# A hybrid attention block on one Trainium2 core: the first block re-ordered from its projections to its masks

## The reference

```python
proj = rms_norm(h, norm_mix) @ w_in          # q, k, v of attention, rw (15 tiles), two gates
y_sb = stick_breaking_attention(q, k, v)     # 8 heads of 64
rw   = token_shift(rw, mu)                   # p + (previous row - p) * mu
r, kr, vr, w_lo, a_lo, g_lo = split(rw)
decay = exp(-exp(-softplus(-(w0 + tanh(w_lo) @ w_up)) - 0.5))
a = sigmoid(a0 + a_lo @ a_up);  g = sigmoid(g_lo) @ g_up
kk = kr * k_k;  kk = kk / max(norm(kk per head), 1e-12)
kr = kr * (1 + (a - 1) * k_a)
y_rw = rwkv7_recurrence(r, decay, kr, vr, kk, a)   # here: blocks of 16, 128, 128 rows
y_rw = (group_norm(y_rw) + sum(r * kr * r_k) * vr) * g
merged = sigmoid(gate_sb) * (y_sb @ w_sb_out) + sigmoid(gate_rw) * (y_rw @ w_rw_out)
h = h + merged @ w_out                        # then the feed-forward part, then block two
```

## Time and profile before

| | us |
|---|---|
| median of 3 runs (2523.31 to 2527.19) | 2525.39 |
| the profiled execution's own time | 2529.52 |
| its span in the profile | 2527.6 |
| PE busy | 2458.6 (97%) |
| DVE busy | 1724.1 (68%) |
| ACT busy | 1252.1 (50%) |
| POOL busy | 537.2 (21%) |

### The profile page before, as it was taken

The page is one execution under the profiler, slowest core; times in us unless marked ns, Lnnn a source line. Parts: engine busy times, 40 slices in busy tenths (PEclk is TensorE's granted clock), DMA queues, the critical chain, the costliest instruction groups (busy, mean ns, idle before and its releaser), DMA issues.

```text
span 2527.6 us, 43738 instructions
## 1 busy us (share of the span) xinstructions
PE 2458.6 (97%) x17339; PEld 2225.9 (88%) x17339; DVE 1724.1 (68%) x3045; ACT 1252.1 (50%) x2676; POOL 537.2 (21%) x423
## 2 busy tenths in 40 slices
PE   7899999999999999999999999999999999999997
PEld 6868998998789999999788878779999999888886
DVE  4647454446669777888777555759876888777556
ACT  5442235445555544444555555555454444555553
POOL 3601134555268300000000001448500000000000
PEclk9989999999999999999999999999999999999999
DMA  5400045565245655555787664335666565787664
GB/s 175 140 12 26 26 145 181 183 186 156 68 134 168 183 184 183 186 180 184 225 246 231 193 206 151 108 102 166 184 184 183 181 185 180 221 245 233 198 196 146
DMA packets 148073, 421.06 MB, mean 167 GB/s; under 512 B 15904, under 2 KB 49056, under 8 KB 147488
## 3 DMA queue, kind: packets, MB, share of 16 engines
q1 hardware_dynamic: 144080, 405.34, 52.2%
q0 software_dynamic: 2192, 8.99, 1.0%
q10 hardware_dynamic: 1600, 3.96, 0.5%
HBM read 400.40 MB, written 17.83 MB: 165 GB/s over the span
## 4 chain that ended last, share of the span: by engine, by line
PE 87%; DVE 6%; DMA 3%; ACT 3%; issue 1%; POOL 0%; ACTq 0%; DVEq 0%; SPq 0%
PE pb L430 86%; DMA raw<-in_vT 3%; PE pb L439 1%; ACT arena L1122 1%; DVE arena L1575 1%; ACT hi L1110 1%; DVE arena L1578 1%; DVE lo L1585 1%; ACT L1122 0%; DVE WL L2270 0%; DMA H<-in_x 0%; DVE arena L2243 0%; DVE arena L1657 0%; DVE arena L1634 0%; DVE H L1575 0%
## 5 line engine op out<-in xcount | busy, mean ns | idle before, releaser
L1110 ACT CAST hi<-raw 128x512 fp32r<-128x512 f32 x1402 | 814.7, 620 | 387.7 <-DMA raw<-in_vT 193.2
L430 PE MATMUL pb<-HTh,hi 128*128 128x256 f32 (+1 forms) x2968 | 857.8, 289 | 0.1
L430 PE MATMUL pb<-HTl,hi 128*128 128x256 f32 (+1 forms) x2968 | 842.3, 284 | 0.0
L430 PE MATMUL pb<-HTh,lo 128*128 128x256 f32 (+1 forms) x2968 | 842.0, 284 | 0.0
L2306 POOL TENSOR_TENSOR lo<-raw,hi 128x512 fp32r<-128x512 f32 x383 | 516.5, 1372 | 595.8 <-ACT hi L1110 595.2
L1585 DVE TENSOR_TENSOR lo<-raw,hi 128x1024 fp32r<-128x1024 f32 x464 | 565.4, 1219 | 83.8 <-ACT hi L1110 83.8
L430 PEld LDWEIGHTS pb<-HTh,hi 128*128 128x128 f32 x2968 | 570.2, 192 | 2.7 <-DVE arena L1575 0.6
L430 PEld LDWEIGHTS pb<-HTl,hi 128*128 128x128 f32 x2968 | 570.6, 192 | 1.0
L430 PEld LDWEIGHTS pb<-HTh,lo 128*128 128x128 f32 x2968 | 569.8, 192 | 0.0
L430 PE MATMUL pb<-hi,WH 128*128 128x512 f32 x1112 | 434.7, 391 | 6.6 <-DVE WL L2270 6.5
L430 PE MATMUL pb<-lo,WH 128*128 128x512 f32 x1112 | 433.5, 390 | 0.0
(11 more groups left out here) (194 smaller groups left out, 2272.0 us busy)
## 6 DMA issues: line engine op xcount, KB each, us to landing
raw<-in_uT SPq DMA_DIRECT2D x256, 512.0 KB, 3.7
raw<-in_vT SPq DMA_DIRECT2D x256, 512.0 KB, 4.3
raw<-in_w_ffn_in SPq DMA_DIRECT2D x44, 512.0 KB, 4.0
raw<-in_wq SPq DMA_DIRECT2D x32, 512.0 KB, 3.6
wk<-kept SPq DMA_DIRECT2D x128, 128.0 KB, 4.3
raw<-in_w_in SPq DMA_DIRECT2D x24, 512.0 KB, 3.7
raw<-in_w_ffn_out SPq DMA_DIRECT2D x22, 512.0 KB, 4.4
raw<-in_w_gate SPq DMA_DIRECT2D x16, 512.0 KB, 3.5
```

Of the source, the lines that this page charges most:

```text
L430: return e.matmul(o, l, r, start=start, stop=stop)
L1110: e.copy(u.hi[k], u.half[k]).then_inc(*s.up("hi", ("hi", g)))
```

## The change

Nothing is computed by another method except two roots and two scalings: the square root and reciprocal of the key norm and of group norm become exp(-0.5 ln(x)) on ACT, and the decays' factor -exp(-0.5) moves from a DVE instruction into the scale of ACT's exps. The squares and the scaled key move from DVE to ACT; the key's `1 + (a-1) k_a` becomes one ACT Identity with a scale and bias (`oka`) per f. The rest is order and banks:

- the small low-rank matmuls go one f at a time behind `rw` tiles 4 to 7, the scans behind DVE's tiles 7 to 10, the head sums `kk_ps` behind tile 10; they use banks 4 to 7 (`SIDE`);
- `gt_ps` goes between q and k, `bv_ps` behind the second k unit, the three transpose groups of VR behind the third;
- scores `att_z` stand before, between and behind the v units; the other six transpose groups go two by two behind the mask stage's gates, all in bank 6;
- five of the 16 gate units go into attention (two ahead of it, three between heads), with a plain copy from PSUM and one later sigmoid for all five; three stay in the masks, eight are left for the solves and the tail;
- `warm` calls: 64 of these matmuls before in this part (7 x 14, 6, 6, 8, 3 x 4, 2 x 4, 10), 12 after;
- the side products come as sbo 0, sbo 1, rwo 0, rwo 1, then in pairs.

The diff, cut to its core:

```diff
+SIDES = [("sbo", 0), ("sbo", 1), ("rwo", 0), ("rwo", 1), ("sbo", 2), ("rwo", 2), ("sbo", 3), ("rwo", 3)]
-GATE_BANK = (6, 7, 6, 6, 7, 0, 1, 2, 3, 0, 1, 2, 3, 0, 1, 2)
+GATE_BANK = (0, 1, 2, 0, 1, 7, 7, 7, 6, 7, 0, 1, 2, 3, 0, 1)
+RAW_GATES = 5
+SIDE = 4
 # tensor
-    for n in range(9):
-        rw_tile(n)
...
+    for n in range(15):
         rw_tile(n)
+        if 4 <= n < 8:
+            lora(n - 4)
+        elif n == 10:
+            head_sums("kk_ps", m.RN, "kk2", "kkn")
...
     for f in range(4):
         b = projected(units.take("k", f), 128, 0, ("k_ps", f))
         free[b] = [("k", f)]
+        if f == 1:
+            head_sums("bv_ps", m.RK, "pr", "bv")
+        elif f == 2:
+            for i in range(3):
+                row_tile(2, i, SIDE + i)
...
-    warm(7, 14)
-    for h in (0, 2):
-        att_z(h)
-        warm(7, 6)
...
+    att_z(0)
+    att_z(2)
+    values(0)
+    att_z(4)
+    values(1)
+    att_z(6)
+    values(2)
+    values(3)
...
+    gate()
+    gate()
+    for h in range(8):
+        att_c(h)
+        if h in (2, 4, 6):
+            gate()
+        if h > 2:
+            att_y(h - 3)
+    for h in (5, 6, 7):
+        warm(2, 4)
         att_y(h)
...
         gate()
+        for k in (2 * i, 2 * i + 1):
+            row_tile(k // 3, k % 3, 6)
...
-    for _ in range(5):
-        gate()
-    warm(7, 10)
+    gate()
 # scalar
+        if 5 <= n < 9:
+            f = n - 5
+            w.wait_ge(*s.to("rw", 1 + f))
+            fn(m.KK[:, f, :], m.KR[:, f, :], ACT.Copy, scale=m.K("k_k", f)).then_inc(*s.up("keys", ("kk", f)))
+            w.wait_ge(*s.to("kk", f))
+            fn(m.RN[:, f, :], m.KK[:, f, :], ACT.Square).then_inc(*s.up("keys", *([("kk2",)] if f == 3 else [])))
...
+    w.wait_ge(*s.to("rw", 14))
+    fn(m.RW[0:32, 14, :], m.RW[0:32, 14, :], ACT.Sigmoid).then_inc(*s.up("loras", ("g2",)))
...
+            fn(m.TMP[3], m.TMP[3], ACT.Ln).then_inc(*s.up("roots", ("kk_ln",)))
+            fn(m.TMP[3], m.TMP[3], ACT.Exp, scale=-0.5).then_inc(*s.up("roots", ("kk_root",)))
+            fn(m.RTf, m.TMP[4], ACT.Exp, scale=-DECAY).then_inc(*s.up("decays", ("decay_r",)))
...
+        if g < RAW_GATES:
+            e.copy(m.GA[:, g, :], PB[GATE_BANK[g]][:, 0:NQ]).then_inc(*s.up("gates_raw", ("ga_raw", g)))
 # vector
-    ts(TMP[0], TMP[0], -float(np.exp(np.float32(-0.5))), None, M).then_inc(*up("decay"))
...
-    e.reciprocal(TMP[3], TMP[3]).then_inc(*up("decay"))
...
+    for n in range(15):
+        shifted(n)
+        if 7 <= n < 11:
+            scan(n - 7)
...
-    e.reciprocal(m.yt2, m.yt2).then_inc(*up("centre"))
```

More of the change, by code:

```diff
@@ L155, in stream @@
         add(("gate", g), d["w_gate"][g], low=pool)
-    for g in range(4):
-        add(("sbo", g), d["w_sbo"][g], cut=False)
-        add(("rwo", g), d["w_rwo"][g], cut=False)
+    for name, g in SIDES:
+        add((name, g), d["w_" + name][g], cut=False)
     for c in range(8):
@@ L510, in tensor, with values @@
         free[b] = [("k", f)]
-    for g in range(4):
+        if f == 1:
[3 more added lines that the diff above has]
+                row_tile(2, i, SIDE + i)
+    def values(g):
         u = units.take("v", g)
@@ L620, in pair_products @@
                     free[b] = [(name, i, par)]
-    gates = iter(range(16))
-    def gate():
-        g = next(gates)
-        b = projected(units.take("gate", g), 128, 16, ("ga_ps", g), GATE_BANK[g])
-        free[b] = [("ga", g)]
     for i in range(3):
@@ L791, in tensor @@
         free[b] = [("yc", b)]
-    for _ in range(3):
+    for _ in range(2):
         gate()
@@ L1323, in mix @@
             e.copy(m.HT[0][:, 2 * g + k, :], m.mt[k][:, 0:256]).then_inc(*s.up("mix_hi", ("mh", g, k)))
-    for g in range(4):
-        if g:
-            mix(g - 1)
-        take("sbo", g)
-        take("rwo", g)
+    for i, unit in enumerate(SIDES):
+        take(*unit)
+        if i in (3, 5):
+            mix(i // 2 - 1)
+    mix(2)
     mix(3)
@@ L1629, in vector @@
+    w.wait_ge(*s.to("km", 3))
     own()
-    ts(TMP[0], TMP[0], -float(np.exp(np.float32(-0.5))), None, M).then_inc(*up("decay"))
-    w.wait_ge(*s.to("const"))
+    tt(TMP[5], TMP[5], m.kr2, M).then_inc(*up("decay"))
+    for f in range(4):
+        take("q", f)
     own()
     for f in range(4):
-        e.tensor_tensor_scan(m.CUM[:, f, :], C("scan"), m.SW[:, f, :], 0.0, M, A).then_inc(*up("decay"))
-    own()
-    for b in range(2):
-        e.tensor_copy(m.CM[:, :, b:b + 1], m.CUM[:, :, 79 + 128 * b:80 + 128 * b]).then_inc(*up("decay"))
@@ L1661, in vector @@
+    tt(m.BTf, m.BTf, m.KTf, M).then_inc(*up("decay"))
+    own()
+    tt(m.KTf, TMP[5], m.KTf, M).then_inc(*up("decay", ("tk",)))
+    for f in range(4):
+        w.wait_ge(*s.to("bv_ps", f))
+        tt(m.BV[:, f, :], PB[SIDE + f][:, 0:NT], m.VR[:, f, :], M).then_inc(*up("decay", ("bv", f)))
+    for f in range(4):
         take("k", f)
@@ L2341, in gpsimd @@
         take("gate", g)
-    for g in range(4):
-        take("sbo", g)
-        take("rwo", g)
+    for unit in SIDES:
+        take(*unit)
     for c in range(8):
```

351 lines of the change are left out of this document (166 added, 185 removed).

## The result

The changed kernel takes 2502.31 us (median of 4 runs, 2496.49 to 2505.64) against 2525.98 us for the one before on the same chip (4 runs, 2523.31 to 2527.19). The ratio is 0.9900, 95% interval 0.9888 to 0.9912: some 25 us less, 22 to 28 by the interval (23.7 between the medians). The forecast was 2497 us with a range of 2491 to 2509; the time lies in it, 5.3 us above the forecast.

The account below looks back on a forecast made before the run. PE was taken to bound the kernel (87% of the chain of waits). Terms -17.3 + 2.5 + 1.8 - 15.1 = -28.1 us gave 2501.4, or 2497 us after 4.1 us for the profiled run's excess; range 2491 to 2509.

Parts of the forecast that it names:

- Gaps, half clock, warms, gates, to attention's end: Projections to attention's end: gaps -11.6, half clock -14.9, warms -5.0, five added gates +14.2; sum -17.3 us.
- +2.5 of stalls: Projections to attention's end: PE held up by late q low halves, last k copy and one join; +2.5 us, bounds 0 and 10.
- The single term of -14.9: Projections to attention's end: work at half clock runs at full clock, 5.4 of it from the transposes; -14.9 us.
- Ln and exp: ACT's key root: program order shows two table loads of 1.28 us; one load would lower the +2.5 by at most 1.3.
- The rival of the low clock: From q to attention's end, small gaps keep PE at 1.2 GHz: +93 us, near 2590 us; chance 0.05.
- Heads' chain covered: Attention: three heads' distance, at least 3 x 2.1 us of PE work, covers a chain of about 0.1 + 0.7 + 0.7 us.
- gates block the heads: Attention: the next head's exp waits on ACT until PE finishes a gate; +8.5 us, 2506 us; chance 0.09.
- Casts late: q units: last shift 5 us late, ACT's casts late, PE stops and meets half clock; +9 us, 2506 us; chance 0.13.
- Masks (+1.8): Masks: the first transpose pair, sharing bank 6, delays the products DVE waits for; +1.8 us, bounds 0 and 5.3.
- Tail (-15.1): Behind the solves: five gates fewer, no warms, group norm's chain hidden by 0.9, last sigmoid 0.3 late; -15.1 us.
- The sign that I gave, eight gates behind the solves: Sign of a right forecast: eight gate units would stand behind the solves.
- Output products: Stage from the first output product to the next norm's table load: forecast difference 0 us.

Follow-up runs that it names:

- the kernel with mix(2) moved: Changed kernel, but ACT takes the cast of the third mixed pair ahead of the cast of the second output unit: 2499.68 us, ratio 0.9896.
- the same order without gates: Changed kernel with none of the five gate units in attention, all five put behind the masks: 2520.03 us, ratio 0.9961.
- the run with two gates: Changed kernel with two gates ahead of the heads, the three between heads moved behind the masks: 2502.29 us, ratio 0.9900.
- the run with late decays: Changed kernel with DVE's scans, maxima and differences put behind tile 14 instead of among the tiles: 2508.03 us, ratio 0.9929.
- the kernel before with its waits filled: Kernel before plus warm matmuls where PE waited, 60 ahead of the key head sums, 14 and 4 x 4 at the bonus sums: 2520.38 us, ratio 0.9980.
- moving the first pair: Changed kernel with the masks' transposes put none, four, two behind the first three blocks' products instead of two each: 2502.16 us, ratio 0.9906.

## Why the prediction was right, by its own steps

- *Gaps, half clock, warms, gates, to attention's end (-17.3, and +2.5 of stalls).* Measured -15.1 against -14.8, and -13.7 without the first four tiles: that the two agree to 0.3 us is in part luck. The gaps closed: PE rests 148.24 - 145.83 = 2.4 us, forecast 3. The last shift was to end near 82 to 83 us; it ended at 82.33, and q's low halves came 0.7 and 1.2 us late, forecast 0.3 and 1. "Where PE never rests the same work runs at full clock" held here; the kernel with mix(2) moved shows that it isn't a law. The single term of -14.9 holds 3.4 for transposes that move to the masks; the clock's own 11.5 stands only together with the closed gaps: by itself, with the order of before, it is 8 us, since there the faster PE meets DVE sooner.
- *Ln and exp.* Two loads, as the order showed: 84.11 and 87.85 us, 1.28 us each, one ahead of ln and one ahead of exp. The page "ScalarE: Activation LUTs" of the Trainium skill (section "Table sets"), by which one would do, does not agree with this program's trace; no run tried it with one.
- *The rival of the low clock.* I gave it 0.05 for 93 us of work at half clock. In the changed order it did not come. In the same order without gates it did, for 42 us and some 15 to 18 us of time, from a wait of 4.2 us. My argument against it ("158.2 to 188.7 ran at 1.00 with heads in close order") was sound as far as it went: heads in close order held the clock when it was high in the run with two gates, and lost it once for a few us in the one with mix(2) moved. What I did not see is that the two gates ahead of the heads are what keeps PE from waiting there; I had them in the sum only as a cost.
- *Heads' chain covered.* Right: between the heads PE has no wait, with gates between them or without, so "gates block the heads" is refuted.
- *Casts late.* Did not happen in the changed kernel (1.9 us of waits); the run with late decays shows a wait of 3.3 us and 3.0 us of time when DVE's order is another.
- *Masks (+1.8).* Measured +1.0, by a mechanism that I had only in part. Each pair waits 0.7 us as forecast, and the stage is DVE's (22.98 of 27.42 us busy). But the masks before had 0.50 from 208 to 214 us, which my rows cut off at 209.5, and the kernel before with its waits filled takes 27.5 us there at 1.00 with no transpose in it. So the 1.0 us isn't shown to be the transposes' price, and moving the first pair earned 0.2 us.
- *Tail (-15.1).* Measured -14.2. The group norm's chain is hidden: DVE is through at 324.45 us. The last gate's sigmoid came 0.9 us late on PE where I had 0.3. (The sign that I gave, eight gates behind the solves, was miscounted: three stand behind the mean, five in the solves.)
- *The step that failed.* Output products: I priced them at nothing. The sides' new order moved the casts of the output weights on ACT ahead of the third mixed pair, and that costs 2.5 us. With it the sum is -25.6, or 2499.8 us, and the measured ratio gives 25.3; the stages' own sum, without the first four tiles, is -24.6. I had gone through ACT's order up to the first rwo product and not behind it.

## What to carry to other kernels

Ask of filler work which wait it fills, not what it costs where it stands: here two units of real work, equal in price at either place, kept a 4 us wait and 42 us of half clock away, while cheap warms that left 2.65 us of the wait did not. Warms that filled a wait of 7.0 us to 0.5 did keep the clock, in the order of before; that speaks for the filling as what counts. Follow a re-ordered list of loads to its last user: an in-order engine that casts what a DMA brings holds up everything queued behind it. And measure once several kernels that differ by nothing that matters, since here falls of the clock in places that no edit touched were worth as much as each of the small edits.

## What the runs showed of the hardware that I had not expected

- The granted clock can stay at 0.50, 1.2 GHz, for 42 us with PE busy 41.57 of 42.00 us. Running sums took 12.11 us for 38 matmuls there, and 8.35 us for 48 at 1.00, so the durations bear the granted clock out. It came back at attention's end, in the kernel without gates between groups of four warms and head products:

```profile
176.76 1.03 PE L434 MATMUL pb<-cst 128*128 128x256 bf16 x4
177.72 1.92 PE L434 MATMUL pb<-arena 128*64 128x256 f32 x6
179.57 1.03 PE L434 MATMUL pb<-cst 128*128 128x256 bf16 x4
180.54 1.14 PE L434 MATMUL pb<-arena 128*64 128x256 f32 x6
```

  The page "TensorE: Matmul & The Clock Gate" of the Trainium skill (section "Part 1: The HAM clock gate") lets sustained work of the engine alone release the clock. This case's trace does not agree: PE worked without rest and nothing was released until then.
- The clock can fall without any wait of PE, in the midst of fp32 matmuls, and come back within 6 us (the kernel with mix(2) moved, 146 to 152 us: 0.74, 0.50, 0.90 with PE busy throughout); the same sequence kept 1.00 in the changed kernel.
- Whose operation begins first matters beside POOL. In the changed kernel a scan on DVE that starts at 66.18 us takes 0.72 us, and POOL's low half from 66.22 us takes 1.75 (1.38 is the mean of all); the four scans of before, beside a POOL without rest, took 1.66 each.
